# Eight of the 96 expert gathers of each layer move into the routing and the gate table

## The chip, the cores and the metric

One core of one Trainium2 chip runs the whole program. The metric is the device time of one execution in microseconds (us); the median of three runs stands for the kernel.

## What is computed

The reference runs a first block (a Hyena layer and an attention layer) and then a second block of two layers. The change touches the last part of each layer of the second block, the expert layer `peer_ffn`, for 256 tokens of width 1024:

```
q = (xc @ wq).reshape(c, PEER_HEADS, 2, half)
sc = jnp.einsum('thid,ikd->thik', q, keys)
top_s, top_i = lax.top_k(sc, PEER_TOPK)
cand_s = top_s[:, :, 0, :, None] + top_s[:, :, 1, None, :]
cand_i = top_i[:, :, 0, :, None] * PEER_NKEYS + top_i[:, :, 1, None, :]
best_s, best_pos = lax.top_k(cand_s.reshape(c, PEER_HEADS, -1), PEER_TOPK)
idx = jnp.take_along_axis(cand_i.reshape(c, PEER_HEADS, -1), best_pos, axis=-1)
gate = jax.nn.softmax(best_s, axis=-1)
act = jax.nn.gelu(jnp.einsum('td,thkd->thk', xc, u[idx]), approximate=False)
return jnp.einsum('thk,thkd->td', gate * act, v[idx])
```

There are 8 heads, 16 chosen experts for each head and token, and 16384 experts, each with a row of `u` and a row of `v`.

## The kernel before

**Two ways to the experts.** 160 of the 256 tokens are dense (`TD`): all 16384 experts are computed for them, as 128 blocks of 128 experts, and a gate table that is zero for experts not chosen selects. The weights come as chunks of 1 MB through a ring of four slots (`wring`, `stream`, line 442), issued by SP. The other 96 tokens (`NG`) are gathered: one gather fetches 128 rows of `u` and `v` together (128 x 2048 float32, 1 MB) by an indirect DMA that POOL issues (`gather_rows`, line 2576) into one of four slots (`GRING`). 96 gathers serve the 96 tokens of a layer.

**A gather's work** is a step of DVE, `gather_step(g)`: it waits until gather g has landed, multiplies its `u` half with the tokens and sums (line 2563), and then, once ACT has made the gate of gather g-1 (`gather_gate`, lines 2553 and 2555), adds the `v` half of gather g-1, times that gate, to the accumulator (line 2568). A slot is free after that. So gather g is issued after step g-3.

**Four stages**, each with its own order by hand:

- *Routing*: PE makes the first product of 60 blocks (30 chunks, line 2459) while DVE finds the chosen experts, first for the tokens 0 to 127, then for 128 to 255 (`route(1)`, a generator; from its fourth piece on one gather step follows each piece). ACT does a GELU for each chunk (line 2616) and frees its bank; the gates stand between these (`ROUTE_GELUS_FROM`). At the end PE turns the tables (line 2471), after DVE's last signal (line 2777).
- *Gate table*: 40 groups of four tokens. For each, DVE (lines 2807, 2810), POOL (2690) and ACT (2642, 2644) build one-hot matrices, PE multiplies them (2495), and ACT (2657) and DVE (2800) take the result out. PE fills in with the first product of 16 blocks (2482). `TABLE_AT` says after which group DVE takes which gather step; POOL issues four groups after the key, ACT makes the gate three groups after it.
- *Main*: 52 blocks, for each a first product (2510) and a second product (2518), one chunk each. DVE makes the gated activations (2832) that the second product takes. `MAIN_AT` says after which block DVE takes which step.
- *Post*: the second product of the 76 kept blocks, two to a chunk (DVE: 2834 and 2836). `POST_AT` says the same as `MAIN_AT`. Then PE adds the gathered part (2546).

In main and post the issue that belongs to a key n of the tables waits until PE has finished block n+1 (`v_used`):

```
for n in range(BLOCKS):
    ...
        pool.wait_ge(v_used, BLOCKS * l + n + 3)
    ...
    if n - 1 in VALUES_AT:
        issue(VALUES_AT[n - 1] + GRING)
```

In the table the loop of POOL ends with group 39:

```
for n in range(GROUPS):
    ...
    if n - 4 in TABLE_AT:
        issue(TABLE_AT[n - 4] + GRING)
```

Of the kernel before, what the change touches and what calls it, by code (L numbers as in the profile page):

```python
# [90 lines left out]
def program(nc, A, out):  # L91
    ctx = ExitStack()
    with ctx:
# [59 lines left out]
        def view(ap, a):  # L153
            return ap.rearrange("p (a b) -> p a b", a=a)
# [2248 lines left out]
        dense = lambda k: h[:, k, NG:T]  # L2403
        kept_pairs = lambda n: G[:, MAIN + MID + 2 * n:MAIN + MID + 2 * n + 2, :].rearrange("p a t -> p (a t)")

        ROUTE_STEPS = 10
        TABLE_STEPS, MAIN_STEPS = 6, 44
        TABLE_AT = {4 + 6 * n: ROUTE_STEPS + n for n in range(TABLE_STEPS)}
        FIRST_MAIN = ROUTE_STEPS + TABLE_STEPS
        MAIN_AT = {j * MAIN // MAIN_STEPS: FIRST_MAIN + j for j in range(MAIN_STEPS)}  # L2410
        FIRST_POST = FIRST_MAIN + MAIN_STEPS
# [138 lines left out]
        def gather_gate(act, l, g):  # L2550

            act.wait_ge(dot_done, DOT0 + GATHERS * l + g + 1)
            act.activation(DOT[:, g:g + 1], DOT[:, g:g + 1], ACT.Gelu)  # L2553
            act.drain()
            act.activation(GW[:, g:g + 1], DOT[:, g:g + 1], ACT.Copy, scale=GG[:, g:g + 1]).then_inc(gate_done, 1)

        def gather_step(v, l, g):

            if g < GATHERS:
                slot = g % GRING  # L2560
                v.wait_ge(rows_landed[slot], 16 * ((GATHERS // GRING) * l + g // GRING + 1))
                u = ROWS_IN[:, slot, 0, :]
                v.scalar_tensor_tensor(u, u, 1.0, XG[set_of(g)], ALU.mult, ALU.mult, accum_out=DOT[:, g:g + 1]).then_inc(dot_done, 1)  # L2563
            if g:
                v.wait_ge(gate_done, GATES0 + GATHERS * l + g)
                v.drain()
                acc = GACC[set_of(g - 1)]
                v.scalar_tensor_tensor(acc, ROWS_IN[:, (g - 1) % GRING, 1, :], GW[:, g - 1:g], acc,  # L2568
                                       ALU.mult, ALU.add).then_inc(acc_done, 1)
# [9 lines left out]
        def peer_scalar(act, l):  # L2579
# [38 lines left out]
            for n in range(EARLY // 2):  # L2618
# [5 lines left out]
                if n == PLANES_AFTER:  # L2624
                    act.wait_ge(planes_done, PLANES0 + 3 * l + 3)
                    act.activation(GG, bank[4][:, 0:GATHERS], ACT.Copy)
                    act.activation(GPL, view(bank[4][:, GATHERS:3 * GATHERS], 2), ACT.Copy).then_inc(planes_ready, 1)
                if 0 <= n - ROUTE_GELUS_FROM < ROUTE_STEPS:
                    gather_gate(act, l, n - ROUTE_GELUS_FROM)
# [16 lines left out]
            def mid_out(e):  # L2646
                b, _ = bank_of(f"mid{l}", 0, e)
                wait_done(act, f"mid{l}", 0, e)
                act.activation(mid_kept(2 * e, 2), view(bank[b][:, 0:2 * TD], 2), ACT.Gelu).then_inc(bank_free[b], 1)
# [3 lines left out]
            for n in range(GROUPS):  # L2653
# [5 lines left out]
                if MID_STEPS * n // GROUPS // (2 * KT) > MID_STEPS * (n - 1) // GROUPS // (2 * KT) and n > 1:  # L2659
                    mid_out(MID_STEPS * n // GROUPS // (2 * KT) - 1)  # L2660
                if n - 3 in TABLE_AT:
                    gather_gate(act, l, TABLE_AT[n - 3])
            mid_out(MID // 2 - 1)
# [12 lines left out]
        def peer_pool(pool, l):  # L2676
            issued = [0]

            def issue(to):
                while issued[0] < min(to, GATHERS):  # L2680
                    gather_rows(pool, l, issued[0])
                    issued[0] += 1

            pool.wait_ge(gidx_ready, GIDX0 + l + 1)
            issue(GRING + ROUTE_STEPS - 1)
            pool.wait_ge(pair_ready, l + 1)
            for n in range(GROUPS):
# [4 lines left out]
                a.then_inc(hot_b, 1)  # L2692
                if n - 4 in TABLE_AT:
                    issue(TABLE_AT[n - 4] + GRING)
            pool.wait_ge(u_done, U0 + MAIN * l + 2)
# [12 lines left out]
        def peer_vector(v, l):  # L2708
# [73 lines left out]
            for n, _ in enumerate(route(1)):  # L2782
                if n == 1:
# [3 lines left out]
                    for g, m in enumerate((NGA, NGB)):  # L2787
                        v.memset(GACC[g], 0.0)
                        v.drain()
                        v.tensor_copy(GACC[g][0:m, :], XG[g][0:m, :])  # L2790
                if 3 <= n < 3 + ROUTE_STEPS:
                    gather_step(v, l, n - 3)
            assert n >= 2 + ROUTE_STEPS, n

# [3 lines left out]
            def gated(b, x):  # L2798
                v.wait_ge(g_in, GIN0 + GROUPS * l + x + 5)
                v.tensor_tensor(G4[:, x, MAIN + MID:, :], sums_of(b)[:, MAIN + MID:, :], G4[:, x, MAIN + MID:, :], ALU.mult)  # L2800
# [15 lines left out]
            for n in range(GROUPS):  # L2816
                if n + 2 < GROUPS:
                    hots(n + 2)
                gated(n % 4, n)
                if n in TABLE_AT:  # L2820
                    gather_step(v, l, TABLE_AT[n])
            v.drain().then_inc(gated_done, 1)
# [343 lines left out]
```

## Time and profile before

| | us |
|---|---|
| median of three runs | 2891.49 |
| lowest and highest | 2882.84 and 2892.65 |
| the profiled execution | 2897.78 |
| its span, first to last instruction | 2896.1 |
| PE busy | 2679.6 (93%) |
| DVE busy | 1904.4 (66%) |
| ACT busy | 929.1 (32%) |
| POOL busy | 368.6 (13%) |
| moved from memory | 642.45 MB, mean 222 GB/s |

In the profiled execution the expert layers lie at 1165 to 1887 us (layer 0) and 2160 to 2876 us (layer 1). In layer 1 the DVE part of the routing that takes gathers begins at 2249, the table at 2313.5, main at 2395.6 and post at 2659. A busy engine is not yet the one that sets the time: what counts in a stage is which engine or transfer the others wait for last. DMA share is the mean busy share of the core's 16 DMA engines.

### The profile page before, as it was taken

The page shows a single profiled execution, that of the slowest core. Times are in us where ns is not written, and L with a number is a line of the kernel's source. Part 1 is how long each engine was busy: PE and PEld are TensorE (multiplying, and loading weights), DVE is VectorE, ACT ScalarE, POOL GpSimd, SP SyncE. Part 2 cuts the span into 40 slices and gives each one's busy share as a digit, 9 for nine tenths or more (in the row PEclk, how much of TensorE's full clock was granted, in tenths as well). Part 3 has the DMA queues.
Part 4 walks back from the last instruction along what each step waited for, and adds up shares of the span by engine and source line. Part 5 has one row for each costly group of instructions (what it writes and reads, how often), then busy time and mean ns, then how long its engine had stood idle before and what let it go on. Part 6 is the DMA issues. An engine that isn't in the chain of part 4 may idle for free.

```text
span 2896.1 us, 46812 instructions
## 1 busy us (share of the span) xinstructions
PE 2679.6 (93%) x17212; PEld 2412.8 (83%) x17212; DVE 1904.4 (66%) x4138; ACT 929.1 (32%) x2023; POOL 368.6 (13%) x421
## 2 busy tenths in 40 slices
PE   8999999999999999998999878889999899998888
PEld 5888888778888788997999877868889889898886
DVE  6888888556665786789644455448857994444552
ACT  4222222334763665215311110035651261111011
POOL 0000000000000000017411122100000192112220
PEclk9999999999999999999999999999999999999999
DMA  7333333223313334595799999823336948999993
GB/s 300 115 115 112 120 125 123 76 89 117 117 44 117 117 118 155 182 377 190 263 377 387 377 386 379 326 99 111 123 131 237 388 172 330 392 384 387 367 406 142
DMA packets 90946, 642.45 MB, mean 222 GB/s; under 512 B 10096, under 2 KB 10480, under 8 KB 14256
## 3 DMA queue, kind: packets, MB, share of 16 engines
q1 hardware_dynamic: 60480, 420.23, 38.7%
q0 software_dynamic: 30320, 220.35, 19.2%
q8 instruction: 82, 1.34, 0.2%
q14 instruction: 64, 0.52, 0.1%
HBM read 639.49 MB, written 1.05 MB: 221 GB/s over the span
## 4 chain that ended last, share of the span: by engine, by line
PE 64%; DVE 14%; DMA 13%; issue 4%; ACT 2%; DVEq 2%; ACTq 0%; POOL 0%; POOLq 0%
DMA arena<-in_experts,arena 13%; PE bank L2518 12%; PE bank L489 10%; PE bank L491 9%; PE bank L490 9%; PE bank L2459 4%; PE bank L2510 4%; DVE arena L2563 2%; PE bank L1671 2%; DVE arena L2810 2%; DVE res L2568 2%; PE bank L2495 1%; PE bank L992 1%; PE bank L981 1%; PE bank L1365 1%
## 5 line engine op out<-in xcount | busy, mean ns | idle before, releaser
L2518 PE MATMUL bank<-arena,wring 128*128 128x160 f32 x4096 | 624.2, 313 | 112.2 <-DVE arena L2832 48.8
L2518 PEld LDWEIGHTS bank<-arena,wring 128*128 128x128 f32 x4096 | 600.1, 200 | 127.9 <-DVE arena L2836 53.9
L2576 POOL DMA_INDIRECT arena<-in_experts,arena x192 | 212.0, 1104 | 1806.3 <-DVE arena L2785 999.4
L473 DVE TENSOR_TENSOR peer_r<-wring,peer_r 128x512 fp32r<-128x512 f32 x440 | 296.4, 698 | 215.7 <-ACT peer_r L468 212.8
L489 PE MATMUL bank<-h_r,peer_r 128*128 128x512 f32 (+1 forms) x1088 | 397.4, 365 | 4.8 <-DVE h_r L503 3.4
L491 PE MATMUL bank<-h_r,peer_r 128*128 128x512 f32 (+1 forms) x1088 | 384.9, 354 | 0.0
L468 ACT ACTIVATE peer_r<-wring 128x512 fp32r<-128x512 f32 x440 | 266.7, 628 | 233.5 <-PE bank L491 228.6
L2563 DVE SCALAR_TENSOR_TENSOR arena<-arena,res 128x1024 f32<-128x1024 f32 x128 | 156.8, 1225 | 275.2 <-DMA arena<-in_experts,arena 273.9
L490 PE MATMUL bank<-h_r,peer_r 128*128 128x512 f32 (+1 forms) x960 | 334.2, 348 | 0.0
L2553 ACT ACTIVATE arena<-arena 128x1 f32<-128x1 f32 x192 | 38.8, 202 | 766.9 <-DVE arena L2563 766.8
L2459 PE MATMUL bank<-res,wring 128*128 128x160 f32 x1920 | 268.2, 303 | 12.8 <-ACT arena L2616 12.8
L2459 PEld LDWEIGHTS bank<-res,wring 128*128 128x128 f32 x1920 | 265.5, 193 | 15.1 <-issue 14.8
L489 PEld LDWEIGHTS bank<-h_r,peer_r 128*128 128x128 f32 x1088 | 207.3, 191 | 49.5 <-issue 16.8
L2510 PE MATMUL bank<-res,wring 128*128 128x160 f32 x1664 | 244.8, 301 | 0.0
L2510 PEld LDWEIGHTS bank<-res,wring 128*128 128x128 f32 x1664 | 234.4, 192 | 0.0
L491 PEld LDWEIGHTS bank<-h_r,peer_r 128*128 128x128 f32 x1088 | 207.1, 190 | 28.5
L490 PEld LDWEIGHTS bank<-h_r,peer_r 128*128 128x128 f32 x960 | 183.2, 191 | 23.4 <-issue 2.4
L2568 DVE SCALAR_TENSOR_TENSOR res<-arena,res 128x1024 f32<-128x1024 f32 x128 | 164.5, 1285 | 13.2
L2563 DVE SCALAR_TENSOR_TENSOR arena<-arena 128x1024 f32<-128x1024 f32 x64 | 78.3, 1224 | 99.0 <-DMA arena<-in_experts,arena 99.0
L2690 POOL TENSOR_SCALAR arena<-const_t,arena 128x128 f32<-128x128 f32 x200 | 138.3, 706 | 29.4 <-ACT arena L2634 20.6
L490 PE MATMUL bank<-res_r,peer_r 128*128 128x256 f32 x416 | 119.0, 286 | 0.0
L1671 PE MATMUL bank<-res,wring 128*128 128x256 f32 x512 | 113.1, 380 | 0.0
(411 smaller groups left out, 4101.2 us busy)
## 6 DMA issues: line engine op xcount, KB each, us to landing
wring<-in_w_peer SPq DMA_DIRECT2D x256, 1024.0 KB
wring<-in_w_proj SPq DMA_DIRECT2D x34, 1024.0 KB
wring<-in_w_hy SPq DMA_DIRECT2D x32, 1024.0 KB
arena<-in_w_ada POOLq DMA_DIRECT2D x16, 1024.0 KB, 5.1
wring<-in_w_out SPq DMA_DIRECT2D x16, 1024.0 KB
wring<-in_w_ada SPq DMA_DIRECT2D x8, 1024.0 KB
wring<-in_w_hyout SPq DMA_DIRECT2D x8, 1024.0 KB
wring<-in_w_q SPq DMA_DIRECT2D x8, 1024.0 KB
```

The lines of the kernel that those rows point to most:

```text
L468: act.activation(SPLIT[:, buf, 0, :], raw_quarter(name, i, j, q), ACT.Copy).then_inc(split_hi, 1)
L473: v.tensor_tensor(SPLIT[:, buf, 1, :], raw_quarter(name, i, j, q), SPLIT[:, buf, 0, :].bitcast(F32), ALU.subtract).then_inc(split_lo, 1)
L489: pe.matmul(out_ap, w_hi, x_hi, start=start, stop=False, **kw)
L490: pe.matmul(out_ap, w_hi, x_lo, start=False, stop=False, **kw)
L491: return pe.matmul(out_ap, w_lo, x_hi, start=False, stop=stop, **kw)
L1671: mm = pe.matmul(bank[b][:, e * T:(e + 1) * T], w[:, (e * KT + k) * P:(e * KT + k + 1) * P], h[:, k, :], start=(k == 0), stop=(k == KT - 1))
L2459: mm = pe.matmul(bank[b][:, e * TD:(e + 1) * TD], w[:, (e * KT + k) * P:(e * KT + k + 1) * P], dense(k), start=(k == 0), stop=(k == KT - 1))
L2510: mm = pe.matmul(bank[b][:, 0:TD], w[:, k * P:(k + 1) * P], dense(k), start=(k == 0), stop=(k == KT - 1))
L2518: mm = pe.matmul(expert_sum(k), w[:, k * P:(k + 1) * P], GP[:, par, :], start=False, stop=True, skip_group_check=True)
L2563: v.scalar_tensor_tensor(u, u, 1.0, XG[set_of(g)], ALU.mult, ALU.mult, accum_out=DOT[:, g:g + 1]).then_inc(dot_done, 1)
L2568: v.scalar_tensor_tensor(acc, ROWS_IN[:, (g - 1) % GRING, 1, :], GW[:, g - 1:g], acc, ALU.mult, ALU.add).then_inc(acc_done, 1)
L2576: pool.indirect_dma_start(ROWS_IN[:, slot, :, :].rearrange("p a c -> p (a c)"), None, A[f"experts{l}"], bass.IndirectOffsetOnAxis(ap=GIDX[ ...
```

## The change

Only the numbers that say which step stands where are changed. Routing takes 12 gather steps instead of 10, the table 12 (after the groups 3, 6, ... 36) instead of 6 (after 4, 10, ... 34), main 38 instead of 44, and post 35 instead of 37.

```
-        ROUTE_STEPS = 10
-        TABLE_STEPS, MAIN_STEPS = 6, 44
-        TABLE_AT = {4 + 6 * n: ROUTE_STEPS + n for n in range(TABLE_STEPS)}
+        ROUTE_STEPS = 12
+        TABLE_STEPS, MAIN_STEPS = 12, 38
+        TABLE_AT = {3 + 3 * n: ROUTE_STEPS + n for n in range(TABLE_STEPS)}
         FIRST_MAIN = ROUTE_STEPS + TABLE_STEPS
         MAIN_AT = {j * MAIN // MAIN_STEPS: FIRST_MAIN + j for j in range(MAIN_STEPS)}
```

DVE at the end of the routing (2563 and 2568 are a gather step; 2764, 2766 and 2770 are the index sums, of which 2770 is the last before DVE's signal):

```order
 L2568 SCALAR_TENSOR_TENSOR res<-arena,res 128x1024
 L2770 TENSOR_REDUCE arena<-arena 128x128
+L2563 SCALAR_TENSOR_TENSOR arena<-arena,res 128x1024
+L2568 SCALAR_TENSOR_TENSOR res<-arena,res 128x1024
 L2764 TENSOR_TENSOR arena<-arena,const_t 128x2048
 L2766 TENSOR_TENSOR arena<-arena 128x2048
+L2563 SCALAR_TENSOR_TENSOR arena<-arena,res 128x1024
+L2568 SCALAR_TENSOR_TENSOR res<-arena,res 128x1024
 L2770 TENSOR_REDUCE arena<-arena 128x128
 L2772 TENSOR_REDUCE arena<-arena 128x8
```

Two more steps stand ahead of the last sums.

DVE in the gate table, from one gather step on, before:

```order
L2563 SCALAR_TENSOR_TENSOR arena<-arena,res 128x1024
L2568 SCALAR_TENSOR_TENSOR res<-arena,res 128x1024
L2807 TENSOR_SCALAR arena<-const_t,arena 128x128
L2810 TENSOR_SCALAR arena<-const_t,arena 128x128 x4
L2800 TENSOR_TENSOR arena<-bank,arena 128x60x4
L2810 TENSOR_SCALAR arena<-const_t,arena 128x128 x4
L2800 TENSOR_TENSOR arena<-bank,arena 128x60x4
L2807 TENSOR_SCALAR arena<-const_t,arena 128x128
L2810 TENSOR_SCALAR arena<-const_t,arena 128x128 x4
L2800 TENSOR_TENSOR arena<-bank,arena 128x60x4
```

and in the changed kernel:

```order
L2563 SCALAR_TENSOR_TENSOR arena<-arena,res 128x1024
L2568 SCALAR_TENSOR_TENSOR res<-arena,res 128x1024
L2807 TENSOR_SCALAR arena<-const_t,arena 128x128
L2810 TENSOR_SCALAR arena<-const_t,arena 128x128 x4
L2800 TENSOR_TENSOR arena<-bank,arena 128x60x4
L2810 TENSOR_SCALAR arena<-const_t,arena 128x128 x4
L2800 TENSOR_TENSOR arena<-bank,arena 128x60x4
L2807 TENSOR_SCALAR arena<-const_t,arena 128x128
L2810 TENSOR_SCALAR arena<-const_t,arena 128x128 x4
L2800 TENSOR_TENSOR arena<-bank,arena 128x60x4
L2563 SCALAR_TENSOR_TENSOR arena<-arena,res 128x1024
L2568 SCALAR_TENSOR_TENSOR res<-arena,res 128x1024
```

One 2800 is one group, so a step now follows every third group instead of every sixth.

POOL at the end of the gate table (2576 issues a gather, 2690 is table work, and the last row holds the issues of main and post). Before:

```order
L2576 DMA arena<-in_experts,arena 128x2048
L2690 TENSOR_SCALAR arena<-const_t,arena 128x128 x15
L2576 DMA arena<-in_experts,arena 128x2048
L2690 TENSOR_SCALAR arena<-const_t,arena 128x128 x2
L2576 DMA arena<-in_experts,arena 128x2048 x77
```

The changed kernel's piece of the difference:

```order
+L2576 DMA arena<-in_experts,arena 128x2048
+L2690 TENSOR_SCALAR arena<-const_t,arena 128x128 x8
+L2576 DMA arena<-in_experts,arena 128x2048
+L2690 TENSOR_SCALAR arena<-const_t,arena 128x128 x7
+L2576 DMA arena<-in_experts,arena 128x2048
+L2690 TENSOR_SCALAR arena<-const_t,arena 128x128 x5
+L2576 DMA arena<-in_experts,arena 128x2048 x70
```

The issues after the table fall from 77 to 70, by seven and not eight: the table has 12 steps and 11 issues, since the key 36 asks for an issue in a group 40 that isn't there.

## Rows read from the trace of the kernel before

**Rows 1.** The page's span in 40 slices of 72.4 us: GB/s moved.
```profile
GB/s 300 115 115 112 120 125 123 76 89 117 117 44 117 117 118 155 182 377 190 263 377 387 377 386 379 326 99 111 123 131 237 388 172 330 392 384 387 367 406 142
```

**Rows 2.** Windows: length; busy PE, PEld, DVE, ACT, POOL; PEclk, DMA share, GB/s.
```profile
1319.90:1405.00 85.10, 75.28 (x578) 73.75 (x579) 78.45 (x238) 48.30 (x140) 75.58 (x106) 0.96 0.47 169
2313.50:2396.00 82.50, 72.64 (x579) 71.11 (x580) 78.82 (x238) 48.36 (x140) 75.62 (x106) 1.00 0.50 178
...
1404.60:1671.00 266.40, 242.80 (x1661) 240.66 (x1660) 121.11 (x181) 33.76 (x139) 44.95 (x43) 0.94 0.93 368
2395.60:2659.00 263.40, 239.01 (x1683) 235.49 (x1683) 124.60 (x187) 34.52 (x141) 48.53 (x43) 0.97 0.95 379
...
2412.00:2659.00 247.00, 222.61 (x1564) 219.09 (x1563) 116.10 (x174) 31.65 (x130) 48.41 (x43) 0.97 0.98 391
...
2760.00:2800.00 40.00, 36.38 (x256) 34.93 (x256) 22.79 (x40) 3.98 (x16) 9.83 (x9) 1.00 1.01 419
```

**Rows 3.** Waits in main of layer 1: total us, times, longest.
```profile
DVE arena L2563 <- DMA arena<-in_experts,arena: 127.2, 42, 7.9
...
PE bank L2518 <- DVE arena L2832: 24.4, 14, 4.5
```

**Rows 4.** Timeline, end of the routing in layer 1: start, length, engine, line, idle before.
```profile
2291.28 1.01 POOL L2576 DMA_INDIRECT arena<-in_experts,arena  x1 [4.93 <-DVE res L2568]
...
2299.19 1.23 DVE L2563 SCALAR_TENSOR_TENSOR arena<-arena,res 128x1024 f32<-128x1024 f32 x1
...
2301.72 2.28 DVE L2770 TENSOR_REDUCE arena<-arena 128x128 f32<-128x2048 f32 x1
...
2312.01 0.87 PE L2471 MATMUL bank<-const_t,arena 128*128 128x128 f32 x6
```

**Rows 5.** Timeline, gate table of layer 1, around one gather step.
```profile
2349.58 1.24 DVE L2563 SCALAR_TENSOR_TENSOR arena<-arena,res 128x1024 f32<-128x1024 f32 x1
...
2352.14 0.39 DVE L2807 TENSOR_SCALAR arena<-const_t,arena 128x128 f32<-128x128 f32 x1
...
2353.74 1.16 PE L2495 MATMUL bank<-arena 128*128 128x128 f32 x8 [1.47 <-DVE arena L2810]
...
2354.57 1.07 POOL L2576 DMA_INDIRECT arena<-in_experts,arena  x1 [0.16 <-issue]
...
2355.27 0.44 DVE L2807 TENSOR_SCALAR arena<-const_t,arena 128x128 f32<-128x128 f32 x1
...
2366.00 1.16 PE L2495 MATMUL bank<-arena 128*128 128x128 f32 x8 [1.20 <-DVE arena L2810]
```

**Rows 6.** Timeline, start of main in layer 1.
```profile
2407.07 1.22 DVE L2563 SCALAR_TENSOR_TENSOR arena<-arena,res 128x1024 f32<-128x1024 f32 x1
...
2411.88 1.00 POOL L2576 DMA_INDIRECT arena<-in_experts,arena  x1 [18.68 <-PE bank L2518]
...
2417.42 2.34 PE L2518 MATMUL bank<-arena,wring 128*128 128x160 f32 x16
2419.43 1.22 DVE L2563 SCALAR_TENSOR_TENSOR arena<-arena,res 128x1024 f32<-128x1024 f32 x1 [7.93 <-DMA arena<-in_experts,arena]
...
2422.34 2.44 PE L2518 MATMUL bank<-arena,wring 128*128 128x160 f32 x16 [0.40 <-DVE arena L2832]
```

**Rows 7.** Timeline of PE: second products and table products after waits.
```profile
1321.97 2.05 PE L2495 MATMUL bank<-arena 128*128 128x128 f32 x8 [2.68 <-POOL arena L2690]
...
2315.56 1.13 PE L2495 MATMUL bank<-arena 128*128 128x128 f32 x8 [2.67 <-POOL arena L2690]
...
2586.74 4.12 PE L2518 MATMUL bank<-arena,wring 128*128 128x160 f32 x16 [3.14 <-DVE arena L2832]
2616.62 3.56 PE L2518 MATMUL bank<-arena,wring 128*128 128x160 f32 x16 [1.86 <-DVE arena L2832]
...
2686.95 13.31 PE L2518 MATMUL bank<-arena,wring 128*128 128x160 f32 x96 [2.52 <-DVE arena L2834]
...
2828.51 36.72 PE L2518 MATMUL bank<-arena,wring 128*128 128x160 f32 x256 [2.84 <-DVE arena L2836]
```

## The prediction

> **What bounds the kernel now.** I read the 40 slices of the page first. The transfers run below 130 GB/s in most slices and at 326 to 406 in two stretches [rows 1]. Those two are the main and post stages of the two expert layers, where weight chunks and gathers come together. The windows [rows 2] show it by stage. In main of layer 1, from 2412 us on, the DMA engines are busy for 0.98 of the time and move 391 GB/s; in the gate table the share is 0.50 and the rate 178. The waits of main [rows 3] name what is late: DVE waits 42 times, 127.2 us in all, for a gather to land, and PE waits 24.4 us for the DVE product that is queued behind such a wait. So main and post are set by how fast the DMA engines deliver. In the table three engines run close together [rows 2]: in 82.5 us DVE is busy for 78.8, POOL for 75.6 and PE for 72.6. The chain there passes through DVE, and PE waits for DVE once after each gather step, 1.47 and 1.20 us in the two cases shown [rows 5]. At the end of the routing DVE has no gap, and PE's turning of the tables starts as DVE ends [rows 4].
>
> So the change takes load from the stages that the DMA engines set and gives it to two stages that DVE sets.
>
> **Part 1, routing.** Two steps more stand in front of DVE's last sums. One step takes 2.53 us, from the start of line 2563 at 2299.19 to the next reduction at 2301.72 [rows 4]. Nothing hides it: the table can start only when PE has the finished tables. Two steps: +5.1 us per layer. The first new step needs the gather that POOL issued at 2291.28; the step would begin at about 2304, 12.7 us later. In main, with the DMA engines as full, a gather issued at 2411.88 had landed by 2419.43, in 7.6 us [rows 6]. So I add no wait; the bounds are 0 and 2 us. On ACT the two new gates come ahead of the GELUs of the last two chunks. Those chunks end before DVE does, so this costs nothing; if the gate of step 11 were late, the last GELU would come late, but still before DVE's signal.
>
> **Part 2, gate table.** Six steps more. A step takes 2.56 us of DVE, 2349.58 to 2352.14 [rows 5]. When DVE doesn't wait, two groups take 3.13 us (2352.14 to 2355.27), so 1.56 per group. Six groups and a step need 6 x 1.56 + 2.56 = 11.9 us; the distance between the PE waits of two such periods is 12.26 us (2353.74 to 2366.00). DVE is thus idle for only 0.3 us in a period. After the change three groups and a step need 7.25 us, against half of 12.26 = 6.13: +1.12 for three groups, 13.4 for 36 of them. By busy time, six steps are 15.4 us less the 6 x 0.3 of idle time, 13.6 us; by busy time alone 15.4. I take +14.2, between 13.4 and 15.4. POOL issues five gathers more there, 1.07 us each [rows 5]: 75.6 + 5.4 = 81.0 us of about 97, hidden behind DVE. ACT gets two short activations per step and has room. The transfers have room as well, and a slot is ordered some five groups, 12 us, before it is used. If DVE's load were gone, PE would be next, at (12.26 - 1.20) / 6 = 1.84 us per group.
>
> **Part 3, main and post.** A gather is 1.05 MB; at 391 GB/s it takes 2.68 us of all DMA engines [rows 2]. How many fewer are issued there? The steps fall by eight, but the issues by seven: the last key of the table is 36, POOL issues four groups later, and there is no group 40. That gather waits for the first issue of main. So 7 x 2.68 = -18.8 us per layer. The best window of the post stage ran at 419 GB/s [rows 2], the poorest main at 368: 17.5 to 19.9 us. Main keeps room for it. From 2412 on it has about 50 blocks left; at 32 PE records a block and 96 records in 13.31 us [rows 7] that is 4.4 us each, so PE needs 222 of the 247 us, and five gathers fewer leave 234. Part of the gain is lost as PE and transfers come closer, for both then wait for each other by turns. The same work took 266.4 us in layer 0 and 263.4 in layer 1 [rows 2]; from these 3.0 us I take a loss of 2.5, within 0 to 6. DVE's step itself, 2.5 us, is hidden there by waits for transfers.
>
> The Trainium skill ("DMA: Bandwidth & Descriptors", Specifications) names a limit of about 358 GB/s from memory for one core, and by it a gather would be worth 2.93 us and seven of them an estimated 20.5. The windows with 391 and 419 GB/s [rows 2] contradict that limit here, and the sum goes by them.
>
> **Part 4, clock.** The table of layer 0 started with PE at the lower clock, eight records in 2.05 us; that of layer 1 didn't, 1.13 [rows 7]. With 5 us more of idle PE ahead of it, layer 1 should start as layer 0 does. The two tables last 85.1 and 82.5 us [rows 2], so up to 2.6; DVE hides some, and I take 1.5 us, once.
>
> **Sum.** Per layer 5.1 + 14.2 - 18.8 + 2.5 = +3.0. Twice that and 1.5 is +7.5 us. The profiled execution took 2897.78 us, 1.68 more than its span and 6.3 more than the median; it would take 2905. Against the median of 2891.49 this gives **2899 us**, +0.26%. Half a per cent, 14.5 us, is about what a measurement of this kernel can tell from no change, so the forecast is no change.
>
> **The rivals.** *The late gather is paid in full* (slower). The gather pushed out of the table is used after block 2, but issued with the next one only when PE has finished block 1. In the kernel before, the first issue of main went out at 2411.88 for a step one block later, landed by 2419.43, and PE went on at 2422.34 with almost no wait [rows 6]. Now DVE needs it at 2407.07, and the second product that ran at 2417.42 would wait until 2422.3: 4.9 us per layer. My sum holds that this is absorbed, since the DMA engines fill up at the same moment as before. If PE's issue-by-issue pace doesn't let them catch up, it adds 2 x 4.9: 2909. This decides from the point where DMA share in main stays below 0.95. For it speaks the share of 0.93 in layer 0.
>
> *The gathers removed were hidden* (slower): if main and post gain only half, the cost of 19.3 stands against 9.4 and gives 2891 + 20 + 1.5, about 2913. Against it: 0.98 DMA share.
>
> *Half clock in the gate table* (slower). A wait of 3.14 us was followed by 16 records in 4.12 us instead of 2.44, and once 1.86 us was enough for 3.56 [rows 7], that is, the lower of the clock's two levels, 1.2 and 2.4 GHz. The table's waits grow from 1.2 to 1.5 us every 12 us to about 2.1 every 7.25. At 1.2 GHz a group would take PE 3.7 instead of 1.84 us, 147 us for 40 groups, against 97: +100 us for two layers, 2999. Against it: granted clock 1.00 in this stage with the shorter waits [rows 2], and a wait of 2.52 us that was followed by 96 records at full speed [rows 7]. The Trainium skill ("TensorE: Matmul & The Clock Gate", HAM oscillation — how this bites in real kernels) warns that waits between short bursts put every burst at half clock, and this is the change's weak point by it.
>
> *The table hides the steps* (faster). If DVE's gain of lead covers them, a step costs only PE's wait after it, 1.4 us: 8.4 instead of 14.2 per layer, 2887. Against it speaks DVE's 78.8 of 82.5 us.
>
> *The gathers' round trip sets main and post* (faster). If issue, landing and step keep their length whatever the load, post takes 4.8 us per step (from 2659 to its last wait at 2828.51 [rows 7], 35 steps) and main 5.6 (247 us, 44 issues), so the change saves 9.6 + 28 us per layer, not 16.3: 43 less in both layers, 2856. Against it: the share of 0.98.
>
> **Chances.** The forecast 0.48, its own spread 2889 to 2909; late gather 0.20; hidden gathers 0.08; half clock 0.04; table hides 0.12; round trip 0.08. The range is 2880 to 2918: it holds the forecast, the late gather, the hidden gathers and the hiding table but for some tails, and leaves out the half clock and the round trip. Faster by over 0.5% (below 2877): round trip and a tail of the hiding table, 0.09. Slower by over 0.5% (above 2906): half clock, hidden gathers, most of the late gather and a tail of the forecast, 0.32. Between: 0.59.
>
> **What would show it.** Routing: DVE's signal 5 us later after the start of `route(1)`, no wait on the gathers of the new steps. Table: about 97 us instead of 82.5 to 85, DVE busy over 0.95, PE waiting about 2 us for line 2810 in every third group, granted clock over 0.95. Start of main: two issues together, a landing wait of DVE one step earlier, and the second product of block 3 about 5 us late. Main and post: 13 and 5 us shorter, DMA share still 0.95 or more. The forecast is wrong if the table grows by less than 10 us, if main and post together shrink by less than 12 or more than 22 us, or if PE runs at half clock in the table.

## The result and the profile after

The changed kernel takes 2868.06 us (median of six runs, 2859.97 to 2871.46) against 2889.4 us before (six runs, 2882.84 to 2892.65). The ratio is 0.9925, with an interval of 0.9906 to 0.9944: faster by 21.3 us. The forecast was 2899 us, no change. The profiled executions spread more than the medians: that of before took 2897.78 us, 8.4 above its median, that of after 2866.43, 1.6 below. Of the 31.4 us between these two, 5.2 lie ahead of the first expert layer, where the kernels don't differ.

The stages can be read from the first and the last start of single lines of PE: routing from the first 2427 to the first 2471, table to the first 2503, main to the last start of 2510, post to the first 2546 of 32 columns (1.9 us after the first 2546 of all). These bounds end main earlier than [rows 2] does: in layer 1 at 2644.3 and not at 2659. All stage times below are made this way, from one profiled execution of each kernel, in us:

| | routing | table | main | post | sum |
|---|---|---|---|---|---|
| before, layer 0 | 152.7 | 86.2 | 256.5 | 227.3 | 722.7 |
| before, layer 1 | 152.7 | 83.6 | 248.7 | 222.7 | 707.7 |
| after, layer 0 | 157.7 | 100.7 | 230.4 | 213.3 | 702.1 |
| after, layer 1 | 157.8 | 101.8 | 229.9 | 212.5 | 702.0 |

The costs came nearly as forecast, +5.1 in the routing and +14.5 and +18.2 in the table. Main and post gave back far more than the 16.3 us per layer of the forecast: 40.1 in layer 0 and 29.0 in layer 1.

The windows of the changed kernel, in the columns of [rows 2]: the table, main of layer 0, main of layer 1, and main of layer 1 from the first issue on.

```profile
2292.00:2393.50 101.50, 79.24 (x581) 74.47 (x580) 93.62 (x256) 51.19 (x153) 91.06 (x111) 0.95 0.53 193
1418.90:1650.00 231.10, 225.65 (x1638) 225.30 (x1638) 104.28 (x161) 30.94 (x126) 41.66 (x37) 0.99 0.95 388
2393.50:2623.50 230.00, 224.79 (x1634) 224.31 (x1634) 103.58 (x159) 30.53 (x124) 39.59 (x37) 0.98 0.96 388
...
2410.00:2624.00 214.00, 208.79 (x1519) 208.31 (x1519) 98.27 (x151) 28.07 (x116) 39.58 (x37) 0.98 0.99 404
```

Main of the kernel before by the same bounds, layer 0 and layer 1:

```profile
1404.60:1661.10 256.50, 237.66 (x1634) 235.94 (x1632) 117.69 (x176) 33.07 (x136) 42.36 (x41) 0.94 0.93 366
2395.60:2644.30 248.70, 229.89 (x1632) 226.96 (x1632) 117.69 (x176) 33.34 (x136) 46.51 (x41) 0.98 0.95 377
```

The last row of the changed kernel stands against the row of 391 GB/s in [rows 2] (390 when that window ends with main). The same DMA engines, at almost the same busy share (0.99 against 0.98), now move 404 GB/s, and PE is busy for 209 of 214 us. In the table DVE is busy for 93.6 of 101.5 us, POOL for 91.1.

The waits of main in layer 1 (total, times, longest). [rows 3] counts up to 2659; up to the end of main, 2644.3, the kernel before has:

```profile
DVE arena L2563 <- DMA arena<-in_experts,arena: 119.2, 39, 7.9
...
PE bank L2518 <- DVE arena L2832: 18.8, 12, 3.1
```

and the changed kernel:

```profile
DVE arena L2563 <- DMA arena<-in_experts,arena: 114.1, 34, 12.5
...
PE bank L2518 <- DVE arena L2832: 5.2, 2, 5.0
```

DVE still waits 114 us for gathers to land, but PE hardly waits for DVE any more: 5.2 us instead of 18.8. DVE now waits while it is ahead of PE. The waits are only part of main's gain. PE also makes the same products in less busy time, 225.7 us instead of 237.7 in layer 0, where the granted clock rose from 0.94 to 0.99, and 224.8 instead of 229.9 in layer 1. The 5.0 us is one single wait, at the start of main, where the change pushed one gather out of the table:

```profile
2409.99 1.00 POOL L2576 DMA_INDIRECT arena<-in_experts,arena  x1 [20.87 <-PE bank L2518]
...
2411.30 0.95 POOL L2576 DMA_INDIRECT arena<-in_experts,arena  x1 [0.31 <-issue]
...
2417.81 1.23 DVE L2563 SCALAR_TENSOR_TENSOR arena<-arena,res 128x1024 f32<-128x1024 f32 x1 [12.55 <-DMA arena<-in_experts,arena]
2420.73 4.54 PE L2518 MATMUL bank<-arena,wring 128*128 128x160 f32 x16 [5.03 <-DVE arena L2832]
```

Two issues go out together, DVE waits 12.55 us, and PE 5.03 with the lower clock behind it (4.54 us for 16 records instead of 2.34). That is the picture that [rows 6] let one expect.

In the chain of waits of before, main of layer 1, one round reads (start, length, what):

```profile
2417.59 2.19 PE bank L2518 x16
2419.82 0.76 issue
2420.57 10.04 DMA arena<-in_experts,arena
2430.63 1.23 DVE arena L2563
...
2433.17 0.33 DVE arena L2832
2433.54 2.44 PE bank L2518 x16
...
2449.83 10.14 DMA arena<-in_experts,arena
```

PE finishes a block at 2419.78, POOL orders a gather 0.8 us later, it lands after 10.04 us, DVE does its step and then line 2832, and PE goes on at 2433.54. From PE back to PE this is 13.8 us. The next landing in the chain took 10.14 us. In all, eight landings in the chain begin in this main, and they take 8.98 to 10.35 us. The same part of the chain of the changed kernel has three:

```profile
2409.99 7.80 DMA arena<-in_experts,arena
...
2556.48 11.64 DMA arena<-in_experts,arena
...
2617.78 11.14 DMA arena<-in_experts,arena
```

Over the whole span the DMA pieces make 13% of the chain before, and 8% in the changed kernel:

```profile
PE 68%; DVE 16%; DMA 8%; issue 3%; DVEq 2%; ACT 2%; ACTq 0%; POOL 0%; POOLq 0%
```

### The profile page after: what moved, and what is told of

It reads as the page before. It is cut to its first block, busy times and chain, and to the rows that moved or that the text cites. A ratio compares the mean times of both kernels' runs of the same rounds, so it can differ in the third digit from the quotient of the medians.

```text
span 2864.8 us, 46812 instructions
## 1 busy us (share of the span) xinstructions
PE 2660.4 (93%) x17212; PEld 2393.3 (84%) x17212; DVE 1904.5 (66%) x4138; ACT 928.2 (32%) x2023; POOL 386.5 (13%) x421
## 3 DMA queue, kind: packets, MB, share of 16 engines
HBM read 639.49 MB, written 1.05 MB: 224 GB/s over the span
## 4 chain that ended last, share of the span: by engine, by line
PE 68%; DVE 16%; DMA 8%; issue 3%; DVEq 2%; ACT 2%; ACTq 0%; POOL 0%; POOLq 0%
PE bank L2518 13%; PE bank L489 10%; PE bank L491 9%; PE bank L490 9%; DMA arena<-in_experts,arena 8%; PE bank L2510 7%; PE bank L2459 4%; DVE arena L2810 3%; DVE arena L2563 3%; PE bank L1671 2%; DVE res L2568 2%; PE bank L992 1%; PE bank L981 1%; PE bank L1365 1%; PE bank L1383 1%
## 5 line engine op out<-in xcount | busy, mean ns | idle before, releaser
L2518 PE MATMUL bank<-arena,wring 128*128 128x160 f32 x4096 | 606.0, 307 | 65.1 <-DVE arena L2836 38.6
L2518 PEld LDWEIGHTS bank<-arena,wring 128*128 128x128 f32 x4096 | 583.7, 196 | 77.8 <-DVE arena L2836 46.2
L468 ACT ACTIVATE peer_r<-wring 128x512 fp32r<-128x512 f32 x440 | 266.6, 628 | 229.0 <-PE bank L491 225.8
L2690 POOL TENSOR_SCALAR arena<-const_t,arena 128x128 f32<-128x128 f32 x200 | 159.2, 810 | 13.8 <-ACT arena L2634 7.8
L2495 PE MATMUL bank<-arena 128*128 128x128 f32 x640 | 90.4, 285 | 43.6 <-DVE arena L2810 24.5
L2495 PEld LDWEIGHTS bank<-arena 128*128 128x128 f32 x640 | 80.4, 195 | 53.6 <-DVE arena L2810 36.5
```

What stands on the lines that cost most here:

```text
L468: act.activation(SPLIT[:, buf, 0, :], raw_quarter(name, i, j, q), ACT.Copy).then_inc(split_hi, 1)
L2495: mm = pe.matmul(bank[4 + b][:, s * P:(s + 1) * P], OHA[:, t, :], OHB[:, t, :], start=True, stop=True)
L2518: mm = pe.matmul(expert_sum(k), w[:, k * P:(k + 1) * P], GP[:, par, :], start=False, stop=True, skip_group_check=True)
```

## The experiments

Two theories stood against each other. **Theory A**: a round trip sets main and post. A gather is ordered when PE has finished a block, lands some 10 us later and is needed a few blocks on; fewer steps per block put more blocks between order and use. **Theory B**: the DMA engines' throughput at that mix sets them, as the prediction held, and a gather was only priced too low.

### Order earlier, move nothing

```
             for n in range(BLOCKS):
+                if n in VALUES_AT:
+                    issue(VALUES_AT[n] + GRING)
                 if n < MAIN - 2 or n % 2:
...
-                if n - 1 in VALUES_AT:
-                    issue(VALUES_AT[n - 1] + GRING)
```

> The kernel before, with one thing changed: in main and post POOL issues the gather of key n ahead of its wait for PE's block n, not after the wait for block n+1, so it goes out as soon as DVE has freed the slot, some 3.5 to 6 us earlier. Same bytes, same steps, same DVE work. Theory A (the gathers' round trip, from PE's finished block to the landing and to the step that needs it, set main and post): main, 256.5 and 248.7 us in the two layers before, falls to 228 to 242, post (227.3 and 222.7) falls by 8 or more, in all 40 to 60 us faster than before. Theory B (the DMA engines' throughput at that mix set it, 391 GB/s): main and post stay within 3 us each, in all within 10 us of before.

Measured: 2823.68 us, ratio 0.975 (0.9696 to 0.9804); main 232.5 and 232.6, post 210.0 and 205.6. It is 70 us faster than the runs of before beside it (2893.91), more than the 40 to 60 expected; post fell by 17 us per layer. Main of layer 0 and post of layer 0, and the largest wait of PE in that main:

```profile
1406.20:1638.70 232.50, 226.50 (x1633) 222.21 (x1633) 121.42 (x180) 34.67 (x138) 50.19 (x43) 1.00 0.99 409
1638.70:1848.70 210.00, 186.55 (x1255) 180.77 (x1253) 109.75 (x189) 20.18 (x77) 32.69 (x35) 0.94 0.95 385
```

```profile
PE bank L2510 <- DMA wring<-in_w_peer: 6.0, 17, 0.4
```

The bytes, the steps and DVE's work are those of before, and the same main is done in 232.5 us at 409 GB/s instead of 256.5 at 366. Theory B in its simple form falls: the engines had not been at their limit. PE no longer waits for DVE in this main, and what is left are short waits for weight chunks.

The edit also puts the order of a gather ahead of the release of weight chunks, so one could think that gathers are only served sooner. They aren't: from issue to landing a gather takes 11.2 us in the median of this main and a chunk 13.0; in main of layer 0 of the changed kernel it is 10.2 and 8.5.

### Order later, in the changed kernel

```
-                if n - 1 in VALUES_AT:
-                    issue(VALUES_AT[n - 1] + GRING)
+                if n - 2 in VALUES_AT:
+                    issue(VALUES_AT[n - 2] + GRING)
```

> The changed kernel with the round trip made longer: the gather of key n is issued after PE's block n+2 instead of n+1. Same bytes, same steps. Theory A: main loses its room, one block of PE (4.3 us) per round of three steps is taken off, main 245 to 265 instead of 230 us; post takes one block more per round of three steps, 35 / 3 x 2.2 = 25 us longer; in all 60 to 110 us slower than the changed kernel. Theory B (throughput): within 10 us, since the slots are filled as often as the DMA engines allow.

Measured: 3019.78 us, ratio to before 1.0459 (1.0417 to 1.05). The two layers: main 278.6 and 269.3, post 245.8 and 241.6. Layer 0, main and post:

```profile
1418.50:1697.10 278.60, 240.61 (x1634) 235.73 (x1633) 102.67 (x158) 30.19 (x124) 36.86 (x36) 0.94 0.83 318
1697.10:1942.90 245.80, 195.81 (x1254) 188.80 (x1253) 108.02 (x187) 19.59 (x75) 37.86 (x35) 0.91 0.84 326
```

The direction is theory A's, and the size is above its range: 152 us instead of 60 to 110. Post grew by 29 to 33 us (25 expected), main by 39 to 48 (15 to 35 expected). In main of layer 0 PE waits 38.0 us for DVE instead of 5.5:

```profile
PE bank L2518 <- DVE arena L2832: 38.0, 20, 9.8
```

and its busy time grows from 225.7 to 240.6 us at a granted clock of 0.94 instead of 0.99. The estimate for main had no term for the clock.

### From main to post, without the table

```
-        TABLE_STEPS, MAIN_STEPS = 6, 44
+        TABLE_STEPS, MAIN_STEPS = 6, 38
```

> The kernel before with MAIN_STEPS 38 instead of 44: six steps move from main to post (43 there), routing and table untouched. Theory A: main falls to about 224 to 232 us as in the changed kernel, post grows by 6 x 4.8 = 29 us and a little more, in all 0 to 20 us slower than before. Theory B with 2.68 us a gather: main 16 us shorter, post 16 longer, in all 0. If main shrinks by over 20 us without any change to the table, the price of a gather in main was mis-sized, whatever the table does.

Measured: 2909.68 us, ratio 1.0049 (1.0021 to 1.0077), 15.8 us slower than the runs of before beside it, as theory A has it; main 222.3 and 221.8, a little under its range, post 268.9 and 264.4. With 38 steps PE runs through main without a gap, whatever the table does:

```profile
1404.20:1626.50 222.30, 221.93 (x1633) 221.62 (x1632) 102.57 (x158) 30.26 (x124) 37.13 (x36) 1.00 0.97 397
1626.50:1895.40 268.90, 205.15 (x1255) 196.93 (x1253) 127.17 (x211) 23.55 (x91) 43.15 (x42) 0.88 0.83 327
```

Six steps cost post 41.6 and 41.7 us, 7 us each, more than the 4.8 of theory A's estimate and far more than 2.68; and post with 43 gathers moves only 327 GB/s. A stage at the limit of its transfers would not get slower per byte.

### The routing part alone

```
-        ROUTE_STEPS = 10
+        ROUTE_STEPS = 12
```

> The routing part of the change alone: ROUTE_STEPS 12, table 6 steps (after groups 4, 10, ... 34), main 44, post 35. Theory A, with the prices measured so far: routing +5.1 us per layer, table and main as before (86.2 and 83.6; 256.5 and 248.7), post 5 to 7 us shorter for each of the two steps taken out (the kernel with 43 steps there grew by 41.6 for six), so 10 to 14 us; in all 10 to 18 us faster than before. With 2.68 us a gather, as the prediction had it, the sum would be 5.4 - 5.1, so no change.

Measured: 2887.83 us, ratio 0.9991 (0.9971 to 1.0012): no difference that can be told, so the expectation missed. By stages it is less of a miss: routing 157.8, post 217.4 and 212.8 (9.9 shorter in each layer, 5 us a step, as expected), table 87.1 and 86.0, main 248.0 and 253.5. Main with 44 steps thus gives 256.5, 248.7, 248.0 and 253.5 in four layers of two kernels that don't differ there. That scatter is as large as what this part gains. By the stages this kernel is 10 us faster than before and by the medians 3.7: the profiled execution of before was a slow one, and the stage times of a single execution hold to a few us only.

### The table part alone

```
         ROUTE_STEPS = 10
-        TABLE_STEPS, MAIN_STEPS = 6, 44
-        TABLE_AT = {4 + 6 * n: ROUTE_STEPS + n for n in range(TABLE_STEPS)}
+        TABLE_STEPS, MAIN_STEPS = 12, 38
+        TABLE_AT = {3 + 3 * n: ROUTE_STEPS + n for n in range(TABLE_STEPS)}
```

> The table part alone: ROUTE_STEPS 10, table 12 steps (after groups 3, 6, ... 36), main 38, post 37. Theory A: routing 152.7, table 100 to 102, main 230 with one PE wait of about 5 us at its start, post as before, 222 to 227. Per layer +14.5 to +18 and -19 to -26, in all 0 to 20 us faster than before. With 2.68 us a gather it would be slower by 5 to 15 us.

Measured: 2873.48 us, ratio 0.9941 (0.9918 to 0.9963); table 101.2 in both layers, main 231.5 and 228.9, post 225.8 and 219.4 (222 to 227 expected). So the table part carries the change, and it is faster by itself, by 18 us against the runs of before beside it (2891.56).

### The late gather undone

```
-        TABLE_AT = {3 + 3 * n: ROUTE_STEPS + n for n in range(TABLE_STEPS)}
+        TABLE_AT = {2 + 3 * n: ROUTE_STEPS + n for n in range(TABLE_STEPS)}
```

> The changed kernel with the table's steps one group earlier (groups 2, 5, ... 35), so that the last issue falls to group 39, inside POOL's loop, and no gather is pushed into main. Theory A: PE's only wait in main (5.03 us, and about 2 us of half clock behind it) goes, main 223.5 to 226 instead of 230, in all 10 to 14 us faster than the changed kernel. Theory B: the wait is absorbed in a stage that transfers set, less than 4 us in all.

Measured: 2858.19 us, ratio to before 0.9871 (0.9815 to 0.9928), 9.9 us below the changed kernel's median; the two intervals overlap, so the stages have to tell. Main is 221.7 in both layers, 8.7 and 8.2 less, and lower than the 223.5 to 226 expected; the total gain just misses its 10 to 14. The last issue of the table now goes out inside it, the first of main serves one step later, and PE goes on without a gap:

```profile
2391.77 1.08 POOL L2576 DMA_INDIRECT arena<-in_experts,arena  x1 [0.17 <-issue]
...
2410.91 0.95 POOL L2576 DMA_INDIRECT arena<-in_experts,arena  x1 [18.06 <-issue]
...
2418.52 1.23 DVE L2563 SCALAR_TENSOR_TENSOR arena<-arena,res 128x1024 f32<-128x1024 f32 x1 [3.94 <-DMA arena<-in_experts,arena]
...
2420.50 2.34 PE L2518 MATMUL bank<-arena,wring 128*128 128x160 f32 x16
```

Post took 218.3 and 210.9, 5.0 more and 1.6 less than in the changed kernel, within what post varies.

### Both mended

The diffs of the first and the last section on the changed kernel.

> The changed kernel with both: keys 2, 5, ... 35 and POOL issuing ahead of the wait for PE. Theory A: main at PE's floor of 224 us, post down from 213 to about 200, 30 to 40 us faster than the changed kernel, ratio to before about 0.98. Theory B: no more than the e3 kernel with keys 2 gives.

Measured: 2818.0 us, ratio 0.9735 (0.9682 to 0.9788); main 221.6 in both layers, post 198.5 and 196.0. That is 50 us below the changed kernel, more than the 30 to 40 expected. Beside the kernel of before with the early order (2823.68) this differs by 5.7 us, 0.2%, and their intervals overlap widely. So once gathers are ordered early, what the change under study brings can no longer be told.

### A version by the prices

```
-        TABLE_STEPS, MAIN_STEPS = 12, 38
+        TABLE_STEPS, MAIN_STEPS = 12, 42
...
-        POST_AT = {MAIN + j * (KEPT - 10) // POST_STEPS: FIRST_POST + j for j in range(POST_STEPS)}
+        POST_AT = {MAIN + j * (KEPT - 3) // POST_STEPS: FIRST_POST + j for j in range(POST_STEPS)}
```

on the kernel with both mended.

> A version built on the prices: issue ahead of the wait for PE, routing and table 12 steps each (groups 2, 5, ... 35), main 42, post 31 steps spread over the 76 blocks but for the last 3 instead of the last 10. With the round trip out of the way the transfers set post: 73 blocks with 0.5 chunk and 0.42 gather each at about 2.5 us a MB come to 170 us, and 7 us of tail, so post 177 to 190 instead of 197 us; main 224 to 230 instead of 221.6 us. In all 15 to 35 us faster than the kernel with keys 2 and early issue (2818 us).

Measured: 2807.49 us, ratio 0.9711 (0.9678 to 0.9743); main 227.4 and 227.6, post 186.9 and 183.9, table 101.9 and 102.9. It is the fastest of all, though only 10.5 us below the kernel with both mended instead of 15 to 35: the stages of main and post came where expected, but main gave back half of what post gained. Here, as already in main with the early order, the transfers are what PE waits for. Main and post of layer 0, and from the waits of post:

```profile
1421.20:1648.60 227.40, 224.40 (x1632) 221.92 (x1632) 116.60 (x174) 32.79 (x134) 52.14 (x41) 1.00 1.00 414
1648.60:1835.50 186.90, 177.44 (x1256) 170.67 (x1254) 94.84 (x171) 17.20 (x65) 26.90 (x29) 1.00 0.97 398
```

```profile
PE bank L2518 <- DMA wring<-in_w_peer: 6.6, 13, 1.3
```

Of the 9.5 us that PE is idle in this post, 6.6 are direct waits for weight chunks, and in main the rate is 414 GB/s.

## Why the prediction was wrong

**Routing, +5.1 us per layer: right.** Measured 5.0 and 5.1, and 5.1 in the kernel with this part alone. A step in front of DVE's last sums has nothing to hide it. No wait for a landing came with it.

**Gate table, +14.2 us per layer: nearly right.** Measured 14.5 and 18.2; the 1.5 us of clock that the prediction added once belong to the 18.2, and in the kernel with the routing part alone the table of layer 1 grew by 2.4 us. The table of layer 1 did start with PE at the lower clock, its first eight records taking 2.05 us instead of 1.13 [rows 7]. What the prediction left out is POOL. Its table work went from 69.2 to 79.6 us in layer 1:

```profile
L2690 POOL TENSOR_SCALAR arena<-const_t,arena 128x128 f32<-128x128 f32 x100 | 69.2, 707 | 13.1 <-ACT arena L2634 10.1 <-PE bank L2495 2.5
```

before, and after:

```profile
L2690 POOL TENSOR_SCALAR arena<-const_t,arena 128x128 f32<-128x128 f32 x100 | 79.6, 810 | 6.7 <-ACT arena L2634 3.7 <-PE bank L2495 2.6
```

With its issues POOL was busy for 91.1 us and not for 81.0 as worked out, so it was no longer well hidden behind DVE's 93.6. How much of the growth is POOL's is not shown: in this table PE waits 14.2 us for DVE, in 11 waits of up to 2.0, and 2.6 us for POOL. DVE was busy for 0.92 of the table, and not for over 0.95 as the prediction's signs have it.

**Main and post, -18.8 + 2.5 = -16.3 us per layer: this step failed.** The prediction read a DMA share of 0.98 at 391 GB/s as the limit, priced a gather at its 2.68 us of transfer and multiplied by seven. The runs show that neither half of that holds. The engines were busy at 0.98 and could still do 404, 409 and 414 GB/s; over the whole of main their share had been 0.93 and 0.95. In place of the 16.3 us the means below give 31.1 per layer, 21.5 in main and 9.6 in post, beyond the 22 at which the prediction called itself wrong. What a step costs depends on where it stands:

| gather steps | main, four values each |
|---|---|
| 44, order as before | 256.5, 248.7, 248.0, 253.5 |
| 38, one gather late | 230.4, 229.9, 231.5, 228.9 |
| 38, none late | 222.3, 221.8, 221.7, 221.7 |
| 44, early order (two values) | 232.5, 232.6 |

From 44 to 38 steps with none late main lost 29.8 us in the mean (251.7 to 221.9), 5 us a step, and then stood at PE's floor. The clock is in this price, and the prediction had no term for it in main: in layer 0 PE waited 18.8 us before and was busy for 237.7, with 38 steps and no late gather it waited 0.4 and was busy for 221.9. Post lost about 5 us a step below 37 steps and gained 7 above. The means give the result back: main -21.5 (251.7 to 230.2), post -9.6 (37 steps: 227.3, 222.7, 225.8, 219.4; 35 steps: 213.3, 212.5, 217.4, 212.8, 218.3, 210.9), routing +5.1 and table +16.3 (of the two layers) come to -9.7 us per layer, 19 in all, against 21.3 measured.

What stands in the place of the throughput is the round trip of 13.8 us. In main the gather that key k orders is used three keys later. Three keys of 44 steps are 3.55 blocks, and the order waits for the block after k, so PE has 2.55 blocks and one first product to do meanwhile: 2.55 x 4.35 + 2.17 = 13.3 us, less than the trip, and with the keys as whole numbers often only 2 x 4.35 + 2.17 = 10.9. With 38 steps it is 3.1 blocks and 15.7 us. In whole blocks, three keys of 44 steps span three blocks in 20 cases (10.9 us) and four in 21 (15.2); with 38 steps they never span fewer than four. The order one block later makes almost all of those 10.9 again. This is an estimate for main from the chain's pieces, where a product of PE takes 2.17 us and a block, with two of them, 4.35; in post POOL waits only for every second block, and the count was not made there. What bears it out are the two runs that change the order's time and no byte: earlier, and main fell by 16 to 24 us; later, and it grew by 39 to 48. The landing itself is not what changed: 10.04 and 10.14 us in the chain of before, 7.80, 11.64 and 11.14 in that of after. From issue to landing, in main of layer 0 of the changed kernel, of the early order and of the late order (times, median us):

```profile
arena<-in_experts,arena POOLq DMA_INDIRECT x37, 10.2
...
arena<-in_experts,arena POOLq DMA_INDIRECT x43, 11.2
...
arena<-in_experts,arena POOLq DMA_INDIRECT x36, 9.5
```

The kernel with the late order has the shortest landings of the three and by far the longest main (278.6 us, against 230.4 and 232.5). Why post costs 7 us for a step above 37 and 5 below was not tried further.

**The late gather: the effect was right, its absorption was wrong.** The prediction named the place, the 4.9 us and the single PE wait. It then held in its sum that a stage set by transfers would make it up. It didn't: mending it took 8.2 and 8.7 us from main, more than the wait alone. With the slow records behind the wait (4.54 us instead of 2.34) it comes to 7.2 of the 8.2 us in layer 1; the rest is open.

**The rivals.** The round trip, which was given 0.08, was the right one. It forecast 2856 us; the 2868 measured are higher mainly because main also paid for the late gather, 8 us per layer, and the table cost 2 us per layer more. That its prices fit as closely as they do is partly luck: it counted five gathers in main at 5.6 us where six steps went at 5. The argument held against it, the share of 0.98, was no argument. Half clock in the table didn't come: the granted clock there was 0.95. Nor did the table hide its steps.

## What to carry to other kernels

A DMA share near 1 doesn't show that the transfers are the limit. Look at when they are ordered: follow a late transfer back in the chain of waits to what released its order, and if that is the progress of the engine that will wait for it, count the work that lies between order and use against the landing time. Ordering the gathers up to two blocks of PE earlier, which moves no work, brought 2.5% here, over three times what the move of eight gathers did, and the cheapest test of such a doubt is a kernel that changes only the place of the order.

## What the runs showed of the hardware

A busy share of 0.98 to 1.00 of the DMA engines went with 391, 404, 409 and 414 GB/s in four kernels, for the same kinds of transfers, so a share of 0.98 left 6% to be had. Over the stretches of main and post shown here the rate divided by the share lies between 383 (main with the late order, 318 GB/s at 0.83) and about 415 GB/s.

POOL's one-hot instructions got slower with the number of DVE's gather steps: 707 ns in the mean with six steps in the table, 810 with twelve, (79.6 - 69.2) / 6 = 1.7 us for each step of 2.5 us. It is so in every kernel here: 704 to 708 ns in the four with six steps, 789 to 811 in the six with twelve. The Trainium skill ("SBUF — State Buffer", SBUF: two separate sides) says that a VectorE instruction with two inputs in SBUF and a GpSimd instruction that reads it exclude each other for their whole length; the longer means agree, though no run here varied that by itself.
